# A two-block transformer kernel: first projection in split form, half refills of two gate slots, the last pair of each expert layer written out, a joined feed-forward up product, and more clock products

## The reference

```python
x = layer 0: alpha * x + even_mixer(x)      # x @ w_in (1024 x 1952), then differential and latent attention, @ w_o
    layer norm, then alpha * x + hier_moe(x)       # router, 32 experts, two for each token, feed-forward width 512
    layer norm
    layer 1: alpha * x + odd_mixer(x)       # x @ w_qkv, neighbourhood attention, @ w_o2
    layer norm, then alpha * x + hier_moe(x), layer norm
# second block, on the same x
u = rms_norm_2(x, norm1_gain); proj = u @ w_in2      # recurrence and retention, @ w_out
u = rms_norm_2(h, norm2_gain)
up = causal_depthwise_conv(u @ ffn_up_w, ffn_conv_w, ffn_conv_b)    # 1024 -> 6144, three taps over the tokens
a_branch, v_branch = split(up, 2)
h = h + (gelu(a_branch) * v_branch) @ ffn_down_w
return rms_norm_2(h, final_norm_gain)
```

## Time and profile before

| | |
|---|---|
| median of 3 runs | 1599.57 us (1599.17 to 1601.21) |
| profiled execution | 1597.99 us, span 1596.1 us |
| mean granted clock of TensorE | 0.986 of full speed |
| PE busy | 1528.6 us, 96% of the span, 8032 instructions |
| DVE, ACT, POOL busy | 526.9 us (33%), 430.9 us (27%), 132.5 us (8%) |
| DMA | 502.5 MB, mean 315 GB/s |

### The profile page before, as it was taken

The page is one execution under the profiler, slowest core; times in us unless marked ns, Lnnn a source line. Parts: engine busy times, 40 slices in busy tenths (PEclk is TensorE's granted clock), DMA queues, the critical chain, the costliest instruction groups (busy, mean ns, idle before and its releaser), DMA issues.

```text
span 1596.1 us, 19750 instructions
## 1 busy us (share of the span) xinstructions
PE 1528.6 (96%) x8032; PEld 901.2 (56%) x8032; DVE 526.9 (33%) x1096; ACT 430.9 (27%) x730; POOL 132.5 (8%) x100
## 2 busy tenths in 40 slices
PE   7979999999999998999999999999999999899997
PEld 3554545454544445975544454544334596699986
DVE  1463311111111113035411111111111477578865
ACT  0251111111111112444111111111111461465554
POOL 0030100000000002842100000000000430000000
PEclk9999999999999999999999999999999999899999
DMA  9521999999999999731699999999999755445410
GB/s 338 196 95 67 399 427 428 429 427 427 428 428 428 429 429 384 267 162 51 263 400 426 429 429 427 427 427 427 429 429 381 273 211 204 166 160 206 163 53 27
DMA packets 69096, 502.50 MB, mean 315 GB/s; under 512 B 4000, under 2 KB 5280, under 8 KB 43552
## 3 DMA queue, kind: packets, MB, share of 16 engines
q1 hardware_dynamic: 68160, 495.17, 75.7%
q0 software_dynamic: 864, 6.29, 1.0%
HBM read 500.40 MB, written 1.05 MB: 314 GB/s over the span
## 4 chain that ended last, share of the span: by engine, by line
PE 81%; DMA 9%; DVE 5%; ACT 2%; issue 2%; SPq 0%; DVEq 0%; ACTq 0%
PE bank L853 25%; PE bank L877 11%; PE bank L1105 9%; DMA ring<-in_w_up 9%; PE bank L823 7%; PE bank L738 7%; PE bank L703 5%; PE bank L685 4%; PE bank L1116 4%; PE bank L837 3%; PE bank L808 2%; PE bank L785 1%; PE bank L797 1%; PE bank L863 1%; DMA ring<-in_w_in 1%
## 5 line engine op out<-in xcount | busy, mean ns | idle before, releaser
L853 PE MATMUL bank<-ring,arena 128*64 128x512 f32 x1536 | 343.9, 603 | 17.9 <-DMA ring<-in_w_up 9.9
L853 PEld LDWEIGHTS bank<-ring,arena 128*64 128x64 f32 x1536 | 114.0, 139 | 241.8 <-issue 241.6
L877 PE MATMUL bank<-ring,arena 128*64 128x512 f32 x768 | 170.1, 595 | 1.3 <-ACT arena L1239 1.3
L1655 DVE TENSOR_TENSOR arena<-arena,bank 128x512 f32<-128x512 f32 x32 | 22.0, 688 | 389.3 <-PE bank L853 389.3
L823 PEld LDWEIGHTS bank<-SEL,x_by_row 128*128 128x128 f32 x1088 | 124.0, 192 | 26.6 <-issue 26.0
L823 PE MATMUL bank<-SEL,x_by_row 128*128 128x128 f32 x1088 | 130.5, 278 | 0.3
L1667 DVE SCALAR_TENSOR_TENSOR y_low<-bank,ST,y_high 128x512 fp32r<-128x512 f32 x64 | 48.1, 751 | 201.2 <-ACT y_high L1243 201.2
L1105 PE MATMUL bank<-x_high,w_high 128*128 128x256 f32 x384 | 109.9, 286 | 2.6 <-DVE x_low L1497 2.6
L853 PE MATMUL bank<-arena 128*64 128x512 f32 x384 | 111.9, 592 | 0.0
L1243 ACT ACTIVATE y_high<-bank,ST 128x512 fp32r<-128x512 f32 x64 | 44.0, 687 | 248.1 <-PE bank L877 248.1
L877 PEld LDWEIGHTS bank<-ring,arena 128*64 128x64 f32 x768 | 53.9, 137 | 100.6 <-issue 100.6
(11 more groups left out here) (306 smaller groups left out, 2257.7 us busy)
## 6 DMA issues: line engine op xcount, KB each, us to landing
ring<-in_w_gate SPq DMA_DIRECT2D x48, 2048.0 KB, 19.5
ring<-in_w_up SPq DMA_DIRECT2D x48, 2048.0 KB, 20.0
ring<-in_w_down SPq DMA_DIRECT2D x48, 2048.0 KB, 18.0
arena<-in_w_gate SPq DMA_DIRECT2D x12, 2048.0 KB, 19.7
arena<-in_w_up SPq DMA_DIRECT2D x12, 2048.0 KB, 19.9
arena<-in_w_down SPq DMA_DIRECT2D x12, 2048.0 KB, 20.6
ring<-in_ffn_up SPq DMA_DIRECT2D x12, 2048.0 KB, 8.4
ring<-in_w_in SPq DMA_DIRECT2D x9, 2048.0 KB, 12.5
```

The lines of the kernel that those rows point to most:

```text
L853: last = nc.tensor.matmul(bank[4 + m][64 * e:64 * e + 64, :], XG[:, c, 64 * e:64 * e + 64], w[e][:, c, :], start=(c == 0), stop=(c == C - 1))
L877: last = nc.tensor.matmul(bank[6 + half][64 * e:64 * e + 64, :], HT[:, j, 64 * e:64 * e + 64], w[e][:, j, 512 * half:512 * half + 512], st ...
```

## The change

1. **First projection.** `x @ w_in` goes through the split form. ACT and DVE make the parts of x (in place of copying it) and of the weights; the weights' parts take two holes in the ring, so SP loads w_uq and w_ukv as before and the first item behind the projection when the projection is done. Three clock products stand ahead of it.
2. **Clock products** also: two after the third scores in each of the two attention stages that share a routine, and one between the differential attention and the 32 transposes.
3. **Router and refill.** Ranks count from 1, so one DVE instruction falls away. RANK, SEL and `rtop` come ahead of the gate weights; the gather comes ahead of the transpose of `rtop`, and the flag is computed after the copy of the first tokens. Behind the first half of pair 0's gate products PE signals `half_used`; SP then loads the first halves of the next matrices into the two gate slots, and their second halves when the gate products are done. The up products of pair 0 wait for the flag.
4. **Last pair.** It is taken out of the loop. It has no gather, no SEL and no copy of gathered tokens. The scatter of pair 14 moves ahead of its transposes. Its own scatter goes by halves of the columns, with three signals, and DVE's statistics wait for one bank each. In the unrolled pairs and in the loop nothing moves.
5. **Feed-forward up.** x_high and x_low lie side by side. One product of 512 columns does w_high with both, into the two halves of a bank, and one of 256 adds w_low x x_high to the first half. ACT copies the first half to SBUF (FSUM) and DVE adds the second; all three taps then read FSUM, and the bank is free when the sum is done (`f_sum`). ACT's order in a tile is copy, high weights, tap 0; DVE's is sum, low weights, taps. In tiles 24 to 47 POOL multiplies gelu's result with the branch, where DVE did.

The diff, cut to its core:

```diff
@@ buffers
-        XHI, XLO = part("x_high", "MT", 0, [P, C, SEQ]), part("x_low", "XT", 0, [P, C, SEQ])
+        XSPLIT = part("x_split", "XT", 0, [P, 2, C, SEQ])
+        XLO, XHI = XSPLIT[:, 0], XSPLIT[:, 1]
+        FSUM = [cut(13312 + 256 * i, SEQ) for i in range(4)]
@@ SP: order of the items, refill
+            if g == 2:
+                ein_holes = hole(pj_done, 2 * G_UQ), hole(pj_done, 2 * G_UQ)
+            I_EIN.append(item(columns(w_in, n, EIN_W[g]), C, EIN_W[g], w_lo, TILES * (g + 1)))
...
+                    if n == POOL:
+                        sp.wait_ge(half_used, l + 1)
+                        for slot_no, m in ((ring_item(l, m - POOL) % RING, m) for m in (n, n + 1)):
+                            sp.dma_start(ring[:, slot_no, 0:SLOT // 2],
+                                         expert_source(l, m // 6 * 2 + m % 2, m % 6)[:, 0:SLOT // 2])\
+                                .then_inc(half_loaded, 16)
@@ POOL, behind all else
+            for g in range(DOWN_T):
+                f = g + DOWN_T
+                pool.wait_ge(f_gelu, g + 1)
+                pool.wait_ge(f_cv, f + 1)
+                nc.gpsimd.tensor_tensor(ACTT[:, g, :], ACTT[:, g, :], CV[f % 4], ALU.mult).then_inc(f_act, 1)
@@ PE, shared attention routine
+                        if i == 2:
+                            keep_clock(7, 2)
@@ PE, experts
+            def scatter_by_half(n):
+                pe.wait_ge(moe["swt_copied"], n + 1)
+                for half in range(2):
+                    for y, ready in ((YHI, moe["y_high"]), (YLO, moe["y_copied"])):
+                        pe.wait_ge(ready, n * 2 + half + 1)
+                        for t in range(T):
+                            last = nc.tensor.matmul(bank[2 * t + half][:, :], SWT[:, t, :],
+                                                    y[:, 512 * half:512 * half + 512],
+                                                    start=False, stop=False, skip_group_check=True)
+                            if y is YLO and half:
+                                last.then_inc(acc_done, 1)
+                    if not half:
+                        last.then_inc(acc_done, 1)
...
+                    if m and up_free is not None:
+                        pe.wait_ge(*up_free)
...
+                        if up_free is not None and (m, c) == (0, C // 2 - 1):
+                            last.then_inc(half_used, 1)
...
-                gather(s, x_rows)
+                if next_pair:
...
+                    gather(s, x_rows)
+                else:
+                    scatter(s, n - 1)
@@ PE, router
+                pe.wait_ge(moe["sel_ready"], PAIRS * l + 1)
+                pe.wait_ge(xp_ready, T * (l + 1))
+                gather(moe, x_by_row)
                 pe.wait_ge(r_top, l + 1)
                 nc.tensor.transpose(bank[5][0:1, 0:P], rtop, ident).then_inc(top_done, 1)
-                pe.wait_ge(moe["sel_ready"], (PAIRS + 1) * l + 1)
-                pe.wait_ge(xp_ready, T * (l + 1))
-                gather(moe, x_by_row)
@@ PE, first projection
-            transposed("x")
-            for g, n in enumerate(EIN):
-                w = min(512, EVEN_IN - 512 * n)
-                project(G_EIN + g, I_EIN[g], x_tile, lambda c: slot(I_EIN[g], C, w)[:, c, :], C)
+            keep_clock(3, 3)
+            for g in range(len(EIN)):
+                split_project(S_EIN, g)
@@ PE, behind the differential attention
+            pe.wait_ge(d_exp, 2 * A_HEADS)
+            keep_clock(7, 1)
@@ PE, feed-forward up
                 if f >= 4:
-                    pe.wait_ge(f_cv, f - 3)
+                    pe.wait_ge(f_sum, f - 3)
                 for c in range(C):
-                    w_high, w_low = WHI[f % WBUF][:, c, :], WLO[f % WBUF][:, c, :]
-                    for n, (w, xs) in enumerate(((w_high, XHI), (w_high, XLO), (w_low, XHI))):
-                        last = nc.tensor.matmul(bank[f % 4][:, 0:SEQ], w, xs[:, c, :], start=(c == 0 and n == 0),
-                                                stop=(c == C - 1 and n == 2))
+                    nc.tensor.matmul(bank[f % 4][:, :].rearrange("p (a b) -> p a b", a=2), WHI[f % WBUF][:, c, :],
+                                     XSPLIT[:, :, c, :], start=(c == 0), stop=False, skip_group_check=True)
+                    last = nc.tensor.matmul(bank[f % 4][:, 0:SEQ], WLO[f % WBUF][:, c, :], XHI[:, c, :],
+                                            start=False, stop=(c == C - 1), skip_group_check=True)
@@ ACT, feed-forward up
+                        act.wait_ge(f_cv, f - 3)
+                    nc.scalar.copy(FSUM[f % 4], bank[f % 4][:, 0:SEQ]).then_inc(f_low, 1)
+                    high_weights(f + WBUF)
+                    act.wait_ge(f_sum, f + 1)
@@ DVE, router (moved up, ahead of the gate weights)
+                link(v.scalar_tensor_tensor(RANK[:, :, 0:EXPERTS], rk, 1.0, ELOG[:, :, :], ALU.add, ALU.mult))
...
+                select(moe, 0, 0)
+                v.tensor_reduce(rtop, RANK[:, :, :].rearrange("p t e -> p (t e)"), AX, ALU.max).then_inc(r_top, 1)
@@ DVE, statistics
+            def expert_stats(l, t):
...
+                    dve.wait_ge(acc_done, 3 * l + (t + 2 if n else 1))
@@ DVE, feed-forward up
             for f in range(FF2_T):
+                dve.wait_ge(f_low, f + 1)
+                v.tensor_tensor(FSUM[f % 4], bank[f % 4][:, SEQ:2 * SEQ], FSUM[f % 4], ALU.add).then_inc(f_sum, 1)
+                low_weights(f + WBUF)
...
-                if f >= DOWN_T:
-                    g = f - DOWN_T
-                    dve.wait_ge(f_gelu, g + 1)
-                    dve.wait_ge(f_cv, f + 1)
-                    v.tensor_tensor(ACTT[:, g, :], ACTT[:, g, :], CV[f % 4], ALU.mult).then_inc(f_act, 1)
-                low_weights(f + WBUF)
```

More of the change, by code:

```diff
@@ L416, in split_tile @@
             i = s["items"][k // TILES]
+            width = s["widths"][k // TILES]
             rows_ = C // TILES
-            return i, slot(i, C, 512)[:, k % TILES * rows_:(k % TILES + 1) * rows_, :], s["bufs"][k % TILES]
+            high, low = (b[:, :, 0:width] for b in s["bufs"][k % TILES])
+            return i, slot(i, C, width)[:, k % TILES * rows_:(k % TILES + 1) * rows_, :], (high, low)
         def split_used(s, k):
@@ L556, in low_tiles @@
                     pool.wait_ge(w_hi, s["k0"] + k + 1)
-                    nc.gpsimd.tensor_tensor(low[:, :, :], src, high[:, :, :], ALU.subtract).then_inc(w_lo, 1)
+                    nc.gpsimd.tensor_tensor(low, src, high, ALU.subtract).then_inc(w_lo, 1)
             def rows_of_x(l):
@@ L752, in operands @@
                     tok = slice(t * P, (t + 1) * P)
-                    high, low = (b[:, c % 2, :] for b in bufs)
+                    high, low = (b[:, c % 2, 0:s["widths"][j]] for b in bufs)
                     return (XHI[:, c, tok], high), (XHI[:, c, tok], low), (XLO[:, c, tok], high)
-                split_products(s, j, tiles, lambda t: [lambda b: b[:, :]], operands, quarters)
+                split_products(s, j, tiles, lambda t: [lambda b: b[:, 0:s["widths"][j]]], operands, quarters)
             def split_project_t(s, j):
@@ L864, in experts @@
                 last.then_inc(s["hT_done"], 1)
-                if not first:
+                if next_pair and not first:
                     scatter(s, n - 1)
@@ L929, in early_matrix @@
                         i = ring_item(l, place) + turn * RING
+                        if POOL <= n < POOL + 2:
+                            pe.wait_ge(half_loaded, 32 * (l + 1))
                         pe.wait_ge(*arrived(i))
@@ L1159, in evac_token @@
                 nc.scalar.copy(XT[:, 0:4, t * P:(t + 1) * P], src).then_inc(tr_act, 1)
-            def evac_by_token(name):
-                for t in range(T):
-                    evac_token(name, t)
             def high_input(name, t, gain=None):
@@ L1273, in high_tiles @@
                     act.wait_ge(*arrived(i))
-                    act.wait_ge(*(s["free"] if k < TILES else split_used(s, k - TILES)))
-                    nc.scalar.copy(high[:, :, :], src).then_inc(w_hi, 1)
+                    if k >= TILES or s["free"] is not None:
+                        act.wait_ge(*(s["free"] if k < TILES else split_used(s, k - TILES)))
+                    nc.scalar.copy(high, src).then_inc(w_hi, 1)
             def next_tiles(s, j, evac):
@@ L1582, in normed, with low_tiles @@
                 v.tensor_scalar(xn[:, t, :], X[:, t, :], rs_l[:, t:t + 1], None, ALU.mult).then_inc(xn_ready, 1)
+            def low_tiles(s, ks):
+                for k in ks:
+                    _, src, (high, low) = split_tile(s, k)
+                    if s["k0"] + k:
+                        dve.wait_ge(w_lo, s["k0"] + k)
+                    dve.wait_ge(w_hi, s["k0"] + k + 1)
+                    v.tensor_tensor(low, src, high, ALU.subtract).then_inc(w_lo, 1)
             def continue_pair(i, a0, dest):
@@ L1777, in _ @@
             link(v.memset(WGT[:, :, :], 0.0))
-            evac_by_token("x")
```

(13 more changed lines are left out.)

159 lines of the change are left out of this document (85 added, 74 removed).

## The result

The changed kernel takes 1588.84 us in the median of 4 runs (1588.36 to 1591.45), the kernel before in the same comparison 1599.88. The ratio is 0.9932 (95% interval 0.992 to 0.9944). It is faster, by 11 us; the forecast was 27, and 1588.84 lies outside its range of 1566 to 1579. The profiled execution took 1588.95 us with a span of 1587.2, 8.9 less than before.

A forecast was written before the change was run, and what follows sets the result against it. PE was busy 96% of the span, with the weight stream binding the expert stages and PE the up projection. 10.0 + 2.1 + 3.0 + 10.1 + 2.0 = 27.2 us off 1597.99 gave 1570.8, median 1572.4; range 1566 to 1579.

The forecast's parts named there:

- Part 1: First projection: starts at 14.5, takes 41.7 us, ends 10.3 us earlier; taken as 10.0 us (8.6 to 10.4).
- Part 2: Clock products: 1.0 before the transposes, 1.4 in neighbourhood attention, -0.3 in the other; together 2.1 us (-0.5 to 3.3).
- Part 3: Router and refill: half loads close a 2.7 us DMA hole, 1.1 returns later; 1.5 a layer, 3.0 us (2 to 6).
- Part 4: Last expert pair: gather gone, scatter moved and halved; 4.9 us in layer 0, 5.2 in layer 1, 10.1 (8.5 to 10.5).
- Part 5: Feed-forward up projection: PE could save 5.0 us, less waits of DVE on POOL; taken as 2.0 us.
- the full lock: Up projection's second half: DVE waits for POOL's whole product, round 3.07 us, 4.1 lost, so a gain of 0.9 us.
- rival A: Up projection: POOL's product, starting beside an addition that reads PSUM, does not hold DVE up; gains 5.0, 1569.4 us; chance 0.15.
- the 2.8 us of slack: Up projection: three tiles of lead, used up after ten tiles; the other 14 lose 0.29 us each.
- The 4.1 us for the lock: Up projection: loss in 14 tiles at 0.29 us each from DVE waiting for POOL, set against a 5.0 us gain.
- the five: Rivals: POOL not holding DVE (0.15), new wait (0.13), smaller stream gain (0.10), DVE-bound slowdown (0.03), slower 512-column product (0.07).
- B: First projection and last pairs: DVE's chain arrives last or half clock returns; some 5 us lost, 1577.4; chance 0.13.

The follow-up runs named there:

- cured_both: Changed kernel with norm rows loaded after the last pair's up products, PE's code shifted by 85 waits and 60 never-run instructions; 1573.47 us, ratio 0.9832.
- the run with both causes removed: Changed kernel with norm rows loaded after the last pair's up products and the never-taken further rounds left out on all engines; 1572.84 us, ratio 0.9825.

## Why the prediction was wrong, point by point

**Part 1, first projection: right.** 14.69 for 14.5, 41.89 us for 41.7, 10.0 us for 10.0. PE, not DVE, ends it. The half clock did not return there: from 12.27 to 15.50 us the granted clock is 1.00, where the earlier trace rows have 0.68.

**Part 2, clock products: right in size where it can be read.** The neighbourhood attention gained 1.5 (lead 5.0 to 6.5; 1.4 forecast). In layer 0, clock and router together gave 1.6 from the projection's end to the first gate product; the prediction's numbers for it are 1.0 - 0.3 for the clock and 0.9 for the gate, 1.6. The three places were not run one by one.

**Part 3, router and refill: right on the place and on the sum, wrong on whose it is.** The halves are issued at 169.13, as the rows of SP's queue show that answer to the earlier trace rows:

```profile
169.13 0.81 SPq L503 DMA_DIRECT2D ring<-in_w_down  x2
172.56 0.88 SPq L518 DMA_DIRECT2D ring<-in_w_down  x2
...
191.59 0.80 SPq L518 DMA_DIRECT2D ring<-in_w_up  x2
```

By the bytes moved, the stream's lead goes from 10.4 to 13.1 and then to 12.1 by 205, with the part of it that comes back later as forecast. In layer 1 it goes from 6.5 to 9.1 and 8.0. That is 1.7 and 1.5 us, forecast 1.5 a layer; the forecast's 10.0 + 0.7 + 1.5 for layer 0 is the 12.2 that was measured. But the prediction puts all of it down to the halves, and without them 1.0 and 0.9 remain: the halves are worth 0.6 to 1.1.

**Part 4, last pair: wrong, and it is the step that failed.** It was to give 10.1 us, and the lead fell by 12.3 there in the changed kernel: from the stream's 12.2 to 5.0, and from its 8.2 to 3.1. Three things were missed.
First, of the gather that goes, the step counted PE's time, not who waits on its semaphore. POOL did; its 1 MB moved into a stream whose share was 1.01, and the last pair's up products started 2.47 us late in layer 0. The step named no queue of POOL's, though the wait's count stands in the diff.
Second, "no DMA wait stands in the chain behind them: from 608.01 on PE is the chain" left out that PE needs its instructions. All versions on top of the change with the block of further rounds and no shift idle 4.1 to 6.2 us behind the last scatter, in both layers. This was not the last pair's own doing. The idle stays with part 4 undone, so the other parts' changes to PE's code are enough to bring it; which of them was not run. Removing the block took 9.9 us; 115 waiting instructions cost the kernel before 15.6 us, 5.4 of them their own, and took 7.5 out of the other.
Third, with both gone it gives 6.2, not 10.1: what PE no longer holds up, ACT's order (0.35 us) and DVE's step beside POOL (1.7 us) do in each layer.

**Part 5, up projection: paces right, the price of the lock wrong.** The part gained 5.9 us in the profiles (140.7 to 134.8), forecast 2.0, between the full lock (0.9) and rival A (5.0). Rival A, with a chance of 0.15, is what came. By the starts of PE's products a tile takes 2.880 us before and 2.773 after (forecast 2.89 and 2.78), and 2.773 holds to the end: 48 x 0.107 = 5.1. The other 0.8 is half clock at the start of the stage, 2.5 us before and 1.7 after. Windows, with the columns of the earlier trace rows: first the stage's start before, then its start and its second half in the changed kernel:

```profile
1380.60:1395.00 14.40, 14.36 (x101) 14.37 (x102) 6.37 (x9) 6.22 (x9) 0.00 (x0) 0.83 0.38 128
```

```profile
1377.20:1391.60 14.40, 14.39 (x75) 12.61 (x76) 7.83 (x13) 7.94 (x13) 0.00 (x0) 0.89 0.44 156
1445.00:1512.00 67.00, 67.00 (x389) 59.13 (x388) 65.00 (x98) 45.91 (x77) 15.67 (x21) 1.00 0.49 178
```

But A came for another reason than it gives: the stretching is there, and partial. DVE's low tiles, first and last of its approach to steady state:

```profile
1452.41 1.34 DVE L2058 TENSOR_TENSOR w_low<-ring,w_high 128x1024 fp32r<-128x1024 f32 x1 [0.30 <-ACT w_high L1474]
...
1463.56 1.71 DVE L2058 TENSOR_TENSOR w_low<-ring,w_high 128x1024 fp32r<-128x1024 f32 x1
```

A low tile takes 1.22 us without POOL and 1.71 with it. POOL's product takes 0.74 us, of which 0.10 falls on the sum, which is not stretched (0.42), and 0.64 on the low tile, which takes 0.49 more. The forecast laid all 0.7 on DVE and had a round of 3.07 us; it is 2.88, so DVE falls behind PE by 0.11 a tile, some 2 us in all, and the 2.8 us of slack outlast the stage. PE never waits (67.00 of 67.00 us). The 4.1 us for the lock is the term that was mis-sized; it cost PE nothing. (which the prediction set beside the lock of operations with two inputs, are of an operation with one tensor input; the low tile has two.)

**Luck.** Part 4, with both causes removed, gives 3.9 us less than forecast, and part 5 gives 3.9 more. That is the main reason why cured_both (1573.47) and the run with both causes removed (1572.84) agree with 1572.4; neither confirms the sum. In the changed kernel itself the 22.4 us that part 4 fell short, less these 3.9, are the miss: 27.2 us were forecast and the profiled span is 8.9 shorter.

**The rivals.** None of the five had either cause. B, a new wait that takes part of the largest gains, named the wrong places and 5 us. With 0.95 on "faster" the sign was right. The range was too narrow: all of its bounds came from engines and weights, none from instructions or from POOL's load.

By the Trainium skill (Runtime: NRT & Kernel Launch, Instruction fetch mechanics) instructions come in blocks of 16 KB, 256 of them, fetched in sequence by a DMA of the engine's own; a taken branch whose target is not in the window waits for a fetch. The runs agree: packets of 16 KB, none in the loops, 4.0 to 6.2 us of idle for one missed jump under a full weight stream. The page gives no price for it, and its rule would have been a rival of its own.

## What to carry to other kernels

When an event goes or moves, list every wait on its semaphore, on all engines and queues, and what each issues; a load released early into a full stream costs its bytes at the stream's rate, at the end of the stream. Code behind a loop or a skipped block has an arrival time of its own: compare the idle marked "issue" behind each taken jump in both profiles, and before a change is judged by its time, shift its code by half a fetch and see whether the time moves. And where PE's part of a tail is cut, look for the next engine's order and for what POOL runs beside DVE there.

## What the runs showed of the hardware that was not expected

- A jump over 367 instructions of PE costs nothing or 4.0 to 6.2 us, by the place of the code alone (the kernel before with and without 115 waiting instructions). A jump over 879 costs the same 6.2. Half clock follows the idle: the ten clock records behind it took 6.42 us for 4.45, and the granted clock is 0.50 from 616 to 618. Which places are good was guessed right from counted instructions in the four kernels that shift the code to learn it; the exact rule, how far ahead of PE's place the fetches reach, was not settled.
- An instruction that only waits for a semaphore already reached took PE 0.11 us: with 115 of them in place of 85 the first transposes start at 13.23 instead of 9.99.
- A DVE operation with two inputs in SBUF that overlapped a POOL operation for 0.64 us was stretched by 0.49 us; beside POOL's long low tiles, one of 1.28 took 3.00.
- Joining two fp32r products of 256 columns into one of 512, whose input is two pieces of 256, saved PE 13 ns a pair: 24 products of 256 took 2.880 us, eight of 512 and eight of 256 took 2.773.
